# A hybrid streaming encoder step on one core: the gate's projection is transposed into another PSUM bank

## The chip, the cores and the metric

The kernel runs on one core of one Trainium2 chip. TensorE (PE in the profile) multiplies and transposes, VectorE (DVE) and ScalarE (ACT) read what it leaves in PSUM, GpSimd (POOL) does small work on SBUF, and SyncE (SP) starts the transfers. They run side by side and wait for each other through semaphores. The metric is the device time of one execution in microseconds (us).

## What is computed

The layer normalizes x, projects it, and runs three mixers side by side. The change lies in the attention part, in its gate `ag`:

```python
h = rmsnorm(x, norm_g)
proj = h @ w_in
aq, ak, av, ag, gq, gk, gv, gg, glr, cv, cgl, cg = jnp.split(proj, offsets, axis=-1)
q = rmsnorm(aq.reshape(B, L, ATTN_HEADS, HEAD_DIM), q_g)
k = rmsnorm(ak.reshape(B, L, ATTN_KV_HEADS, HEAD_DIM), k_g)
y_attn = band_attention(q, k_all, v_all, sinks, q_pos0) * jax.nn.silu(ag)
y_gla, y_conv = ...
y = jnp.concatenate([y_attn, y_gla, y_conv], axis=-1) @ w_out
return x + y
```

There are 2048 prompt frames and 64 sample frames of width 1024. Matmuls are made in pieces of a high and a low part (`hi`, `lo`) of each operand: hi·hi + hi·lo + lo·hi.

## The kernel before

The work has two passes. The first makes the attention (projections q, k and v, gate, softmax, its half of the output projection) for 17 tiles of 128 frames, `t.n` from 0 to 16 (`LAST`). The second, from about 500 us on, makes the other two mixers for blocks of 256 frames. Nothing of the second pass is touched.

In the first pass each engine has its own `body_a(t)`, called for t = -2 to 17; its code order is its order of work, and only semaphores tie the engines together. PSUM has eight banks: `J` 0 to 2 for projections and outputs, `S` 0 and 1 for scores and the attention's result, `T` 0 to 2 for transposes. TensorE's order in a tile t is:

1. transposes of q (`qkn`) into `T[2]` (L1808) and of k into `T[0]` (L1810);
2. the first half of the q projection of tile t+1, 12 matmuls 512 wide (L654);
3. four transposes of the gate's projection `agraw` (L1821), which this text calls the gate transposes;
4. the other 12 matmuls of that projection;
5. `scores(0)` and `scores(1)` (L1838), the k/v projection of t+1, `scores(2)` and `scores(3)`, the gate projection of t+1 (24 matmuls);
6. `pT(0)`: probabilities into `T[0]` (L1871); `pX()`: the middle probabilities into `T[1]` (L1880);
7. `out(0)` for tile t-1 (12 matmuls, L669), `pv(0)` (L1894 to L1896), `pT(1)` into `T[2]`, `spread_rinv(t + 2)` into `T[1]` (L591), `out(1)`, `pv(1)`.

`spread_rinv` transposes the spread norm factor of a later tile into `T[1]`; ScalarE copies it out in `take_rinv` (L596) and adds 1 to `rb_taken`. After transposes of q, ScalarE copies the high part out of `T[2]` (`qT`, L958), and VectorE subtracts it to make the low part (L1303, adding 1 to `qk_lo` for each of two halves). They do the same for k from `T[0]` (L1062, L1259). Then come v (L968, L1311), the tanh of the gate on ScalarE (L972), and on VectorE the last low part of y of the tile before (L1250) and the gate's product (L1320, `gate_ready`). Only then does VectorE add the bias and take the maxima of the scores (L1270, `nmx` in L1276), on which ScalarE's exponentials (L988) wait. After the softmax's division (L1360) VectorE makes two steps of the next tile's q/k norm (L1368, L1370), and then the low parts of the transposed probabilities (`ptlo`, L1377, and `px`, L1383), on which `pv(0)` waits.

Of the kernel before, what the change touches and what calls it, by code (L numbers as in the profile page):

```python
# [24 lines left out]
ALU = mybir.AluOpType  # L25
ACT = mybir.ActivationFunctionType
# [7 lines left out]
P = 128  # L34
# [5 lines left out]
TILES = SEQ // P + 1  # L40
# [68 lines left out]
def need(eng, sem, count):  # L109

    if isinstance(count, int) and count <= 0:
        return
    eng.wait_ge(sem, count)
# [7 lines left out]
def groups(b):  # L121

    if b < 0 or b >= NB:
        return []
    return [(0, 0, 256, (0, 1)), (1, 256, DEC, (2,))] if b == 0 else [(b + 1, 0, 256, (0, 1))]
# [67 lines left out]
def build(nc, ins, consts, x_T, outs):  # L193
# [7 lines left out]
    def sb(name, shape, dt=F32, ctx=es):  # L201
        return ctx.enter_context(nc.sbuf_tensor(name, shape, dt))

    def sem(name):
        return es.enter_context(nc.semaphore(name))

    with es:
# [33 lines left out]
        agraw = sb("agraw", [P, 512], F32, ea)  # L241
        gth = sb("gth", [P, 512], F32, ea)
# [82 lines left out]
        T = [es.enter_context(nc.psum_tensor(f"T{i}", [P, 512], F32)) for i in range(3)]  # L325
# [36 lines left out]
        rb_psum, rb_taken, x_normed = sem("x_rinv_psum"), sem("x_rinv_taken"), sem("x_normed")  # L362
# [7 lines left out]
        qk_hi, qk_lo = sem("qkT_hi"), sem("qkT_lo")  # L370
        gate_psum, gate_tanh, gate_ready = sem("gate_psum"), sem("gate_tanh"), sem("gate_ready")
# [249 lines left out]
        def key_slots(t):  # L621

            return slice(0, 3, 2) if t.par == 0 else slice(1, 2)
# [10 lines left out]
        def half_rows(i):  # L634

            return slice(i * HD, (i + 1) * HD)
# [286 lines left out]
        def _(act):  # L923
# [9 lines left out]
            def body_a(t):  # L933
# [20 lines left out]
                if t.real():  # L954

                    act.wait_ge(qk_psum, 2 * t.n + 1)
                    for i in range(2):
                        nc.scalar.activation(qT[half_rows(i), :, :, i, :],  # L958
                                             T[2][half_rows(i), :].rearrange("p (h c q) -> p h c q", c=2, q=CHUNK),
                                             ACT.Copy).then_inc(qk_hi, 1)  # L960
                    act.wait_ge(qk_psum, 2 * t.n + 2)
                    if t.n == LAST:
                        act.wait_ge(c_psum, 1)
                    key_hi(slice(0, P), key_slots(t))
                    if t.n == LAST:
                        key_hi(slice(P, 2 * P), slice(1, 2))
                    act.wait_ge(A.taken[1], t.n + 1)
                    nc.scalar.activation(vcat[t.par][:, :, 0:HD], raw[:, 640:768].rearrange("p (h d) -> p h d", d=HD),  # L968
                                         ACT.Copy).then_inc(v_hi, 1)
                    act.wait_ge(gate_psum, t.n + 1)  # L970
                    need(act, y_gated, 2 * t.n)
                    nc.scalar.activation(gth[:, :], T[2][:, :], ACT.Tanh, scale=0.5).then_inc(gate_tanh, 1)  # L972
                    act.wait_ge(v_lo, t.n + 1)
                    for c, src in enumerate((vcat[t.par], vcat[1 - t.par])):
                        nc.scalar.activation(vdup[c][half_rows(1 - c), :, :], src[half_rows(c), :, :],
                                             ACT.Copy).then_inc(v_dup, 1)
# [46 lines left out]
                if t.real():  # L1023
# [6 lines left out]
                    for u in P_ACT:  # L1030
                        nc.scalar.activation(unit(u), unit(u), ACT.Copy,
                                             scale=rden[:, u:u + 1]).then_inc(p_ready[1], 1)
# [24 lines left out]
            def key_hi(cols, slots):  # L1057

                for g in range(KVH):
                    for o in range(2):  # L1060
                        dst = kT[half_rows(o), g, o, slots, :]
                        nc.scalar.activation(dst, T[0][half_rows(g), cols].unsqueeze(1).to_broadcast([HD, dst.shape[1], P]),  # L1062
                                             ACT.Copy).then_inc(qk_hi, 1)

            def cache_v_hi():

                nc.scalar.activation(vcat[1][:, :, 0:HD], ckv[:, 1, :].rearrange("p (h d) -> p h d", d=HD),
                                     ACT.Copy).then_inc(cv_hi, 1)

            over_tiles(act, body_a)  # L1070

            def o_square(g):
# [96 lines left out]
            for b in range(NB + 1):  # L1169
# [47 lines left out]
                if b == NB - 1:  # L1217
                    g = groups(b)[0]
# [10 lines left out]
        def _(dve):  # L1229
# [32 lines left out]
            def body_a(t):  # L1262
                t1, t2 = t + 1, t + 2

                def scores_max(n):

                    for c in range(2):
                        u = 2 * n + c
                        cols = slice((2 - c) * CHUNK if t.n == 0 else 0, BAND)
                        nc.vector.tensor_tensor_reduce(  # L1270
                            out=unit(u)[:, cols], in0=S[n % 2][:, c * BAND:(c + 1) * BAND][:, cols],
                            in1=bias[:, n, cols], scale=1.0, scalar=sinks[:, n:n + 1],
                            op0=ALU.add, op1=ALU.max, accum_out=mx[:, u:u + 1]).then_inc(s_max, 1)

                def scores_neg(n):
                    nc.vector.tensor_scalar(nmx[:, 2 * n:2 * n + 2], mx[:, 2 * n:2 * n + 2], -1.0, None,  # L1276
                                            ALU.mult).then_inc(s_neg, 1)
# [37 lines left out]
                if t.real():  # L1315

                    need(dve, pt_psum, 3 * t.n)
                    dve.wait_ge(s_psum, 4 * t.n + 1)
                    dve.wait_ge(gate_tanh, t.n + 1)
                    nc.vector.scalar_tensor_tensor(gth[:, :], gth[:, :], 1.0, T[2][:, :], ALU.add,  # L1320
                                                   ALU.mult).then_inc(gate_ready, 1)
                    scores_max(0)
                    dve.wait_ge(s_max, 8 * t.n + 2)
                    dve.wait_ge(s_psum, 4 * t.n + 2)
                    scores_neg(0)
                    scores_max(1)
                    dve.wait_ge(s_max, 8 * t.n + 4)
                    scores_neg(1)
# [102 lines left out]
                if t.fixed and t.n == 0:  # L1431
                    split_lo(A, 3 * KT, 3 * KT + STAGES)

            over_tiles(dve, body_a)

            def history(b):
# [202 lines left out]
            for b in range(NB + 1):  # L1639
# [93 lines left out]
                elif b == NB - 1:  # L1733
                    g = groups(b)[0]
# [32 lines left out]
        def _(pe):  # L1767
# [19 lines left out]
            def body_a(t):  # L1787
# [16 lines left out]
                if t.real():  # L1804
                    need(pe, pt_lo, 4 * t.n)
                    pe.wait_ge(n_step, 4 * t.n + 4)
                    for n in range(PAIRS):
                        last = nc.tensor.transpose(T[2][:, n * P:(n + 1) * P], qkn[:, n * P:(n + 1) * P], ident[:, :])  # L1808
# [7 lines left out]
                if t1.real() and t.n > 0:  # L1816
                    project(A, t1, 0, empty_bank("in", t1.n, 0), 0)
                if t.real():
                    pe.wait_ge(qk_lo, 6 * t.n + 2)
                    for j in range(4):  # L1820
                        last = nc.tensor.transpose(T[2][:, j * P:(j + 1) * P], agraw[:, j * P:(j + 1) * P],  # L1821
                                                   ident[:, :])
                    last.then_inc(gate_psum, 1)
                if t.n == LAST:
# [35 lines left out]
                def p_wait(u):  # L1860
                    e = 1 if u in P_ACT else 0
                    mine = (P_DVE, P_ACT)[e]
                    pe.wait_ge(p_ready[e], len(mine) * t.n + mine.index(u) + 1)

                def pT(g):
                    if g == 1:
                        pe.wait_ge(gate_ready, t.n + 1)
                    for n in (2 * g, 2 * g + 1):
                        for c in range(2):
                            p_wait(2 * n + c)  # L1870
                            last = nc.tensor.transpose(T[2 * g][:, c * 256 + n % 2 * P:c * 256 + n % 2 * P + P],  # L1871
                                                       sc[:, n, c * 256:c * 256 + P], ident[:, :])
                    last.then_inc(pt_psum, 1)

                def pX():
                    pe.wait_ge(rb_taken, min(t.n + 2, TILES))
                    for n in range(PAIRS):
                        p_wait(2 * n)
                        p_wait(2 * n + 1)
                        last = nc.tensor.transpose(T[1][:, n * P:(n + 1) * P], sc[:, n, P:2 * P], ident[:, :])  # L1880
                    last.then_inc(pt_psum, 1)
# [22 lines left out]
                if t.real():  # L1904
                    pT(0)
                    pX()
                out(0)
                if t.real():
                    pv(0)
                    pT(1)  # L1910
                when(t + 2, spread_rinv)
                out(1)
                if t.real():
                    pv(1)

            over_tiles(pe, body_a)

            def project_v(b, i):
# [331 lines left out]
```

## Time and profile before

| | |
|---|---|
| median of 3 runs | 1002.54 us (1002.08 to 1003.2) |
| profiled execution, its own time | 1004.64 us |
| its span, first to last instruction | 1002.9 us |
| mean granted TensorE clock | 0.968 of full speed |
| TensorE busy | 929.5 us (93%) |
| VectorE, ScalarE, GpSimd busy | 790.3, 474.3, 201.1 us |
| 16 DMA engines | q1 26.5% of their span |

The profile is one execution. Busy time alone does not tell what sets the end; the timeline (what ran when, with the idle time before an instruction and who ended it in brackets) and the waits do. TensorE's matmuls overlap: a matmul 512 wide is shown as 0.40 us long while the next starts 0.23 us after it. So a true stall is read from start to start.

### The profile page before, as it was taken

The numbers are of one execution on the slowest core, as the hardware profiler recorded it, in microseconds if no ns is written. First come the engines' busy times: TensorE is split into PE (matmuls) and PEld (weight loads), VectorE is DVE, ScalarE is ACT, GpSimd is POOL, SyncE is SP. The second block draws the span as 40 slices with busy tenths as digits, with TensorE's granted clock in tenths as the row PEclk, the third lists the DMA queues.
The fourth block names the chain that finished last, engine by engine and source line by source line (L and its number), as shares of the span: only waits on it lengthen the run. The fifth ranks groups of instructions, "written<-read, shape, count | busy, mean of one in ns | idle before, by whom it ended". The sixth has DMA issues, their size and how long they took to land.

```text
span 1002.9 us, 15973 instructions
## 1 busy us (share of the span) xinstructions
PE 929.5 (93%) x5713; PEld 818.5 (82%) x5713; DVE 790.3 (79%) x1905; ACT 474.3 (47%) x1166; POOL 201.1 (20%) x250
## 2 busy tenths in 40 slices
PE   5759999999999999998997987999999999999987
PEld 4647888888888888886986886998989898998965
DVE  6578878887888787879878668788888887888974
ACT  7366666666666666657634143041422415142311
POOL 0412222222222222220021221020202112120310
PEclk9879999999999999999999788999999999999989
DMA  9323222222223222135332103204021211203021
GB/s 303 123 97 118 106 106 95 106 106 106 106 106 106 105 106 85 65 111 137 104 107 74 44 22 106 84 1 126 1 89 38 75 53 53 75 8 120 1 74 55
DMA packets 57839, 87.79 MB, mean 88 GB/s; under 512 B 10048, under 2 KB 34496, under 8 KB 57760
## 3 DMA queue, kind: packets, MB, share of 16 engines
q1 hardware_dynamic: 57760, 86.77, 26.5%
q8 instruction: 46, 0.75, 0.3%
q14 instruction: 33, 0.27, 0.1%
HBM read 60.21 MB, written 26.60 MB: 87 GB/s over the span
## 4 chain that ended last, share of the span: by engine, by line
PE 65%; DVE 22%; ACT 5%; issue 3%; DMA 2%; POOL 1%; SPq 1%; POOLq 0%; DVEq 0%; ACTq 0%
PE J L1783 17%; PE J L654 16%; PE J L1942 9%; DVE acc L1460 6%; PE J L669 4%; PE J L1927 4%; DVE osum L1395 3%; PE S L1838 3%; DVE osum L1391 2%; DVE qT L1303 2%; ACT olo L1004 2%; DVE wlo L470 1%; PE S L2096 1%; DVE ptlo L1377 1%; PE T L1821 1%
## 5 line engine op out<-in xcount | busy, mean ns | idle before, releaser
L1460 DVE SCALAR_TENSOR_TENSOR acc<-ub,cwh,acc 128x256 f32<-128x256 f32 (+1 forms) x480 | 224.1, 531 | 0.2
L654 PE MATMUL J<-whi,xhi 128*128 128x512 f32 (+1 forms) x408 | 151.1, 370 | 10.5 <-DVE wlo L470 10.5
L1783 PE MATMUL J<-xbh,whi 128*128 128x256 f32 (+1 forms) x512 | 151.8, 296 | 4.5 <-issue 4.5
L1783 PE MATMUL J<-xbl,whi 128*128 128x256 f32 (+1 forms) x512 | 148.0, 289 | 0.0
L1783 PE MATMUL J<-xbh,wlo 128*128 128x256 f32 (+1 forms) x512 | 147.7, 289 | 0.0
L654 PE MATMUL J<-wlo,xhi 128*128 128x512 f32 (+1 forms) x408 | 147.0, 360 | 0.0
L654 PE MATMUL J<-whi,xlo 128*128 128x512 f32 (+1 forms) x408 | 146.9, 360 | 0.0
L1783 PEld LDWEIGHTS J<-xbh,whi 128*128 128x128 f32 x512 | 98.8, 193 | 7.6 <-issue 7.1
L1783 PEld LDWEIGHTS J<-xbl,whi 128*128 128x128 f32 x512 | 98.8, 193 | 0.2
L1783 PEld LDWEIGHTS J<-xbh,wlo 128*128 128x128 f32 x512 | 98.7, 193 | 0.0
L654 PEld LDWEIGHTS J<-whi,xhi 128*128 128x128 f32 x408 | 78.0, 191 | 22.3 <-DVE xlo L612 9.9
L654 PEld LDWEIGHTS J<-whi,xlo 128*128 128x128 f32 x408 | 77.5, 190 | 12.6
L654 PEld LDWEIGHTS J<-wlo,xhi 128*128 128x128 f32 x408 | 78.0, 191 | 10.3
L988 ACT ACTIVATE sc<-sc,nmx 128x192 f32<-128x192 f32 x136 | 60.2, 445 | 19.5 <-DVE nmx L1276 19.5
L1270 DVE CUSTOM_DVE_ANT_0 sc<-S,bias,sinks 128x192 f32<-128x192 f32 (+2 forms) x136 | 50.2, 406 | 19.3 <-PE S L1838 19.3
L669 PE MATMUL J<-whi,yhi 128*128 128x512 f32 x136 | 56.5, 415 | 0.0
L669 PE MATMUL J<-wlo,yhi 128*128 128x512 f32 x136 | 53.7, 395 | 0.0
L669 PE MATMUL J<-whi,ylo 128*128 128x512 f32 x136 | 53.6, 394 | 0.0
L602 POOL TENSOR_TENSOR xraw<-xraw,rb 128x1024 f32<-128x1024 f32 x17 | 40.8, 2400 | 46.3 <-ACT rb L596 46.3
L885 POOL TENSOR_TENSOR oms<-oss,eps_h 128x8 f32<-128x8 f32 (+1 forms) x9 | 4.9, 549 | 179.9 <-DVE oss L1473 179.0
L1927 PE MATMUL J<-whi,xbh 128*128 128x272 f32 x136 | 40.9, 301 | 0.0
L1927 PE MATMUL J<-whi,xbl 128*128 128x272 f32 x136 | 40.2, 296 | 0.0
(270 smaller groups left out, 2270.3 us busy)
## 6 DMA issues: line engine op xcount, KB each, us to landing
out<-res SPq DMA_DIRECT2D x60, 256.0 KB, 2.0
x_normed_scratch<-xraw SPq DMA_DIRECT2D x17, 512.0 KB, 2.9
xraw<-xT SPq DMA_DIRECT2D x16, 512.0 KB, 3.5
xtok<-in_x_prompt SPq DMA_DIRECT2D x16, 512.0 KB, 3.6
res<-in_x_prompt SPq DMA_DIRECT2D x16, 512.0 KB, 4.5
xbraw<-x_normed_scratch SPq DMA_DIRECT2D x16, 512.0 KB, 5.1
res<-out SPq DMA_DIRECT2D x14, 512.0 KB, 4.2
wraw<-in_w_in SPq DMA_DIRECT2D x52, 128.0 KB, 2.5
```

The costliest lines, as they stand in the source:

```text
L602: nc.gpsimd.tensor_tensor(xraw[t.par][:, :, :], xraw[t.par][:, :, :], rb[:, :].unsqueeze(1).to_broadcast([P, KT, P]), ALU.mult).then_inc(x ...
L654: last = nc.tensor.matmul(bank[:, 0:width], x[x_slot(ps, t)][:, k, :], w, start=(k == 0 and n == 0), stop=(k == KT - 1 and n == 2))
L669: last = nc.tensor.matmul(bank[:, :], y[:, k, :], w, start=(k == 0 and n == 0), stop=(k == 3 and n == 2))
L988: last = nc.scalar.activation(unit(u), unit(u), ACT.Exp, bias=nmx[:, u:u + 1], accum_out=esum[:, u:u + 1])
L1004: nc.scalar.activation(olo[:, :], S[g][HD:P, :], ACT.Copy).then_inc(o_low, 1)
L1270: nc.vector.tensor_tensor_reduce(out=unit(u)[:, cols], in0=S[n % 2][:, c * BAND:(c + 1) * BAND][:, cols], in1=bias[:, n, cols], scale=1.0, ...
L1395: nc.vector.scalar_tensor_tensor(osum[:, 2 * g:2 * g + 2, :], osum[:, 2 * g:2 * g + 2, :], 0.5, gth[:, 256 * g:256 * g + 256].rearrange("p ...
L1460: nc.vector.scalar_tensor_tensor(acc[:, j, 0:frames], src, w, acc[:, j, 0:frames], ALU.mult, ALU.add).then_inc(conv_step, 1)
L1783: last = nc.tensor.matmul(bank[:, 0:w], wt, x[:, k, 0:w], start=(k == 0 and m == 0), stop=(k == KT - 1 and m == 2))
L1838: last = nc.tensor.matmul(S[n % 2][:, c * BAND:(c + 1) * BAND], qT[:, n, c, :, :].rearrange("p e q -> p (e q)"), band(t, n // 2, o, c), st ...
L1927: last = nc.tensor.matmul(bank[:, 0:B.widths[1]], x[:, k, at:at + P], wt, start=(k == 0 and m == 0), stop=(k == KT - 1 and m == 2))
L1942: last = nc.tensor.matmul(bank[:, :], y[:, k % 2, at:at + P], wt, start=(k == 0 and m == 0), stop=(k == 3 and m == 2))
```

## The change

Every tile's gate transposes go to `T[1]` in place of `T[2]`, and the two readers follow. Three waits of TensorE move with them.

```diff
@@ scalar engine
                     act.wait_ge(gate_psum, t.n + 1)
                     need(act, y_gated, 2 * t.n)
-                    nc.scalar.activation(gth[:, :], T[2][:, :], ACT.Tanh, scale=0.5).then_inc(gate_tanh, 1)
+                    nc.scalar.activation(gth[:, :], T[1][:, :], ACT.Tanh, scale=0.5).then_inc(gate_tanh, 1)
@@ vector engine
-                    nc.vector.scalar_tensor_tensor(gth[:, :], gth[:, :], 1.0, T[2][:, :], ALU.add,
+                    nc.vector.scalar_tensor_tensor(gth[:, :], gth[:, :], 1.0, T[1][:, :], ALU.add,
                                                    ALU.mult).then_inc(gate_ready, 1)
@@ tensor engine
                 if t.real():
-                    pe.wait_ge(qk_lo, 6 * t.n + 2)
+                    pe.wait_ge(rb_taken, min(t.n + 2, TILES))
                     for j in range(4):
-                        last = nc.tensor.transpose(T[2][:, j * P:(j + 1) * P], agraw[:, j * P:(j + 1) * P],
+                        last = nc.tensor.transpose(T[1][:, j * P:(j + 1) * P], agraw[:, j * P:(j + 1) * P],
                                                    ident[:, :])
                     last.then_inc(gate_psum, 1)
...
                 def pT(g):
-                    if g == 1:
-                        pe.wait_ge(gate_ready, t.n + 1)
                     for n in (2 * g, 2 * g + 1):
...
                 def pX():
-                    pe.wait_ge(rb_taken, min(t.n + 2, TILES))
+                    pe.wait_ge(gate_ready, t.n + 1)
                     for n in range(PAIRS):
```

No instruction is added, removed or put in another order on any engine; only waits and the bank differ.

## Rows read from the trace of the kernel before

**Rows 1.** The page's busy time of each engine in us.

```profile
PE 929.5 (93%) x5713; PEld 818.5 (82%) x5713; DVE 790.3 (79%) x1905; ACT 474.3 (47%) x1166; POOL 201.1 (20%) x250
```

**Rows 2.** Waits: whole span, then 113 to 440 us; total us, times, longest us.

```profile
PE T L1821 <- DVE qT L1303: 14.4, 16, 2.3
...
PE T L1821 <- DVE qT L1303: 8.5, 12, 0.7
```

**Rows 3.** Timeline of TensorE around the gate transposes of tile 9.

```profile
285.25 0.40 PE L654 MATMUL J<-wlo,xhi 128*128 128x512 f32 x1
285.48 0.40 PE L654 MATMUL J<-whi,xlo 128*128 128x512 f32 x1
286.58 0.66 PE L1821 MATMUL T<-ident,agraw 128*128 128x128 f32 x4 [0.71 <-DVE qT L1303]
287.00 0.48 PE L654 MATMUL J<-whi,xhi 128*128 128x512 f32 x1
```

**Rows 4.** Timeline of tile 9: VectorE, TensorE's first scores, ScalarE's copy of the factor.

```profile
285.12 1.41 DVE L1303 TENSOR_TENSOR qT<-T,qT 64x512 fp32r<-64x512 f32 x2
286.56 1.25 DVE L1259 TENSOR_TENSOR kT<-T,kT 64x128 fp32r<-64x128 f32 x4
...
289.50 0.42 DVE L1250 TENSOR_TENSOR ylo<-osum,yhi 128x256 fp32r<-128x256 f32 x1 [1.37 <-ACT yhi L1054]
290.56 0.69 DVE L1320 SCALAR_TENSOR_TENSOR gth<-gth,T 128x512 f32<-128x512 f32 x1 [0.64 <-PE S L1838]
...
289.88 1.03 PE L1838 MATMUL S<-kT,qT 128*128 128x192 f32 x8
...
279.62 0.27 ACT L596 ACTIVATE rb<-T 128x128 f32<-128x128 f32 x1
```

**Rows 5.** Timeline of tile 10 on VectorE, ScalarE and TensorE.

```profile
312.73 1.78 DVE L1259 TENSOR_TENSOR kT<-T,kT 64x256 fp32r<-64x256 f32 x4
...
316.69 0.69 DVE L1320 SCALAR_TENSOR_TENSOR gth<-gth,T 128x512 f32<-128x512 f32 x1
...
325.89 0.82 DVE L1370 TENSOR_REDUCE qss<-qkn 128x10 f32<-128x640 f32 x1
327.46 0.69 DVE L1377 TENSOR_TENSOR ptlo<-T,pthi 128x512 fp32r<-128x512 f32 x1 [0.76 <-ACT pthi L994]
328.18 1.41 DVE L1383 TENSOR_TENSOR px<-T,px 64x512 fp32r<-64x512 f32 x2
...
318.29 0.46 ACT L988 ACTIVATE sc<-sc,nmx 128x192 f32<-128x192 f32 x1 [0.50 <-DVE nmx L1276]
...
316.01 1.03 PE L1838 MATMUL S<-kT,qT 128*128 128x192 f32 x8
...
326.63 0.60 PE L1880 MATMUL T<-ident,sc 128*128 128x128 f32 x4
329.86 0.28 PE L1894 MATMUL S<-pthi,vcat 128*128 128x256 f32 x1
```

**Rows 6.** Timeline of tiles 0 to 2 on TensorE, and VectorE's gate product of tile 1.

```profile
42.76 1.11 PE L1821 MATMUL T<-ident,agraw 128*128 128x128 f32 x4 [2.01 <-DVE qT L1303]
...
75.89 0.66 PE L1821 MATMUL T<-ident,agraw 128*128 128x128 f32 x4 [2.29 <-DVE qT L1303]
...
89.81 0.90 PE L1871 MATMUL T<-ident,sc 128*128 128x128 f32 x4 [0.29 <-DVE sc L1360]
...
103.64 0.66 PE L1821 MATMUL T<-ident,agraw 128*128 128x128 f32 x4 [0.91 <-DVE qT L1303]
...
79.86 0.69 DVE L1320 SCALAR_TENSOR_TENSOR gth<-gth,T 128x512 f32<-128x512 f32 x1 [0.63 <-PE S L1838]
```

**Rows 7.** Busy time by stretch: us, PE, PEld, DVE, ACT, POOL, granted clock, DMA, GB/s.

```profile
40.70:47.60 6.90, 4.89 (x15) 3.96 (x15) 3.36 (x7) 5.46 (x12) 0.00 (x0) 0.51 0.71 232
...
71.50:470.80 399.30, 381.69 (x2187) 325.30 (x2186) 323.24 (x845) 265.58 (x689) 93.85 (x116) 1.00 0.31 105
```

**Rows 8.** Timeline of TensorE: `pv(0)` of tile 15.

```profile
460.95 0.38 PE L1894 MATMUL S<-pthi,vcat 128*128 128x256 f32 x1 [0.26 <-DVE px L1383]
```

## The prediction

> **What bounds the kernel now.** I read the page's busy times first: TensorE is busy in 93% of the span, VectorE in 79% [rows 1]. That alone only says that TensorE is the one to watch. The waits say more. In the regular part of the first pass, 113 to 440 us, TensorE has one wait in the whole list: the gate transposes wait for VectorE's low part of q, 12 times for 12 tiles, 8.5 us in all [rows 2]. So TensorE sets the pace there, and each stall of it lengthens the span unless another wait takes it over. Over the whole span this wait comes 16 times for the 17 tiles, 14.4 us [rows 2]; tile 16 has none, since a whole projection of the second pass stands before its gate transposes.
>
> The reason lies in the bank. `T[2]` still holds q when the gate transposes come, and VectorE reads it until 286.53 in tile 9 (285.12 + 1.41) [rows 3, 4]. The transposes start at 286.58. How much is lost? The view shows 0.71 us idle, but a matmul's end is drawn later than the moment at which the next can start: two matmuls here start 0.23 us apart and are drawn 0.39 to 0.40 long [rows 3]. The last matmul before the gap starts at 285.48, so the transposes could have started at 285.71. The loss is 286.58 - 285.71 = 0.87 us per tile, not 0.71.
>
> **The removed wait.** The reader is to follow TensorE 0.87 us ahead of itself in tile 9 and ask at each later step whether its input is there.
>
> The new wait of the gate transposes is for ScalarE's copy of the spread factor. It ends at 279.89 [rows 4], 5.82 us before 285.71. It costs nothing, and would do so until the copy came 5.82 us later.
>
> `scores(0)`, at 289.88 now, would start at 289.01. It needs the low part of k, done at 287.81 in tile 9 [rows 4]. Tile 10 has two slots of k to fill and is the tighter one: k is done at 314.51, the scores start at 316.01 and would start at 315.14 [rows 5]. 0.63 us are left. The wait does not move here.
>
> VectorE's product of the gate then waits 0.64 us for the scores in tile 9 and not at all in tile 10 [rows 4, 5]. So VectorE gives 0.64 us of the 0.87 in odd tiles and nothing in even ones: in these, the softmax comes 0.87 us later with respect to TensorE. I therefore keep tile 10's VectorE and ScalarE where they are in time, and move TensorE alone. Behind the gate product stand the maxima, the first exponential at 318.29, and the rest of ScalarE's chain; VectorE ends this stretch with the q/k norm's reduction at 326.71 (325.89 + 0.82) [rows 5]. It starts that after it has made the last probabilities, so these are ready some 1.6 us earlier (two steps of 0.82), at about 325.1. `pX` moves from 326.63 to 325.76: 0.6 us to spare.
>
> Next are the transposed probabilities. `ptlo` waits 0.76 us for ScalarE now [rows 5]. It starts at 327.46, would be due at 326.59, and VectorE is free at 326.71: about 0.13 us late. `ptlo` and `px` take from 327.46 to 329.59 now, 2.13 us, so from 326.73 they end at 328.86. `pv(0)` would be due at 329.86 - 0.87 = 328.99 [rows 5]. It fits, with 0.1 us or less after the 0.05 us that a semaphore takes (286.53 to 286.58 in tile 9 [rows 3, 4]). From here on VectorE is again timed by TensorE and the next tile starts as before.
>
> So a middle tile gains the whole 0.87 us, but an even tile has nearly nothing left over. Tiles 3 to 14: 12 x 0.87 = 10.4 us.
>
> **The other two waits that move.** `pX` now waits for `gate_ready`. The gate product is done at 291.25 in tile 9 and 317.38 in tile 10, over 8 us before `pX` [rows 4, 5]; it would have to be 8 us late to cost anything. `pT(1)` no longer waits for it, which gives nothing for the same reason. Behind `pX` are queued `out(0)`, `pv(0)` and all else of TensorE, so a late gate would be dear, but it is not late. ScalarE's tanh comes right behind the gate transposes and waits for them now; the copies after it wait for VectorE's v, so its earlier start is worth nothing. POOL's and SP's queues are not touched.
>
> **The edge tiles.** Here the price is less plain. Tile 2 stalls 0.91 us in the view; with the same 0.16 us that the view hides (0.87 - 0.71) it is 1.07 [rows 3, 6]. I count 1.07.
>
> Tile 1 stalls 2.29 us in the view [rows 6]. Its gate product waits 0.63 us for the scores [rows 6], so the softmax can come 0.63 us earlier at once, and `pT(0)` at 89.81 already waits for it. The whole 2.3 cannot pass. The lower bound is 0.63, the upper 2.3; part of the softmax in this tile hangs on the later scores, which do come earlier, and I take 0.9.
>
> Tile 0 stalls 2.01 us [rows 6], and all behind it waits for the scores. The lower bound is about 1.1: from 40.7 to 47.6 us the granted clock is 0.51, which is the 1.2 GHz level [rows 7], so work brought forward into this stretch runs at half speed. The stall's end at 42.76 lies inside. If the 2.0 us are filled with work at half speed, only half of it is gained. If the clock rises sooner because TensorE did more, the gain could be 2.8. I take 2.0.
>
> On this the Trainium skill's page "TensorE: Matmul & The Clock Gate", section "What's actually happening", says that the gated state is the default and that activity releases it. The trace agrees in kind: with TensorE busy in 381.69 of 399.30 us the clock stays at 1.00, 2.4 GHz, from 71.5 to 470.8 us [rows 7]. By that rule tile 0 would give the 2.8 and the sum below would be 0.8 us larger.
>
> Tile 15 ends differently: VectorE and ScalarE also split the second pass's first weights there, and `pv(0)` already waits 0.26 us for `px` [rows 8]. So only what the gate product gives, 0.64 us as in the other odd tiles [rows 4], gets through. Tile 16 gives 0.
>
> **The sum.** 10.4 + 1.07 + 0.9 + 2.0 + 0.64 = 15.0 us. The second pass and its transfers start from work that moves as a whole, so the gain is kept to the end. The profiled execution took 1004.64 us, its sum is 989.6. The median of the runs is 2.1 us lower, 1002.54, so I predict 987.5 us.
>
> **Rivals.**
>
> *VectorE closes in even tiles.* The margin before `pv(0)` in tile 10 is 0.1 us or less, worked out from rounded rows. If something I have not seen is 0.3 us longer, six even tiles give 0.6 in place of 0.87: 1.6 us less. In the extreme they give nothing, 6 x 0.87 = 5.2 less: 992.7 us. For it speaks that VectorE runs without a pause from the gate product to the second set of maxima; against it, that it then waits for TensorE's `scores(2)` in every tile, which absorbs small delays. Chance 0.13 for between 989.5 and 993.
>
> *The wait moves to the low part of k.* Then TensorE stands before `scores(0)`. With 0.63 us of margin this needs k 0.63 us later than now; 1.5 us later, all is given back and the time is 1002.5. Nothing in the change makes k later. Chance 0.04.
>
> *The change gives more.* If the clock rises sooner in tiles 0 and 1, both gain in full: 0.8 and 1.4 us more, 985.3. If stretches at half clock in the second pass fall more favourably, another 1 us. Chance 0.13 for below 986.
>
> *Slower: the new wait bites.* The gate transposes now wait for ScalarE's copy of the spread factor, the last but few of its steps in a tile. If that copy came later than the low part of q does today, TensorE would stand longer than before. It decides at 286.53 - 279.89 = 6.64 us of delay; each us beyond costs 1 us in 12 or more tiles, so 1 us beyond gives about 1015. Against it: the copy hangs only on TensorE's own transpose, issued a whole `out(1)` and `pv(1)` earlier. Chance 0.02.
>
> *No effect* because TensorE's clock is granted less when it has no pauses: filling the gaps raises the busy share, and if each tile had one stretch of 1.7 us at half clock the 0.87 would be used up. The row from 71.5 to 470.8 shows no such fall at a busy share of 96% [rows 7], so 0.02 is what I leave it.
>
> **How the numbers follow.** Forecast (986 to 989.5) 0.66, more gain 0.13, less gain by VectorE 0.13, wait moved to k 0.04, clock 0.02, slower 0.02. A measurement of this kernel can tell about 0.2%, 2 us, from no change. The first three cases are all faster by over 1%; k gives half faster, half the same. So faster 0.94, same 0.04, slower 0.02. The range of 8 in 10 cuts the tails of the second and third: 984.8 to 991.5 us.
>
> **What would show it right or wrong.** In the profile after: no wait before the gate transposes in tiles 1 to 15, and these 0.23 us after the matmul before; tiles 25.26 us apart in the middle, where they are 26.13 now (316.01 - 289.88 [rows 4, 5]); the gate product no longer waiting for the scores in odd tiles (0.64 to 0); `ptlo`'s wait falling from 0.76 towards 0 in even tiles; no new wait at `scores(0)` or `pv(0)`. A wait of `pv(0)` on `px` in even tiles would show the first rival, one of `scores(0)` on `kT` the second. In tile 1 I expect a larger wait at `pT(0)`, 0.29 + 1.5 or so. The prediction is wrong if any of these new waits adds up to more than 3 us over the pass.

## The result

| | before | after |
|---|---|---|
| median | 1002.74 us (1002.08 to 1003.2, 4 runs) | 986.45 us (983.97 to 987.71, 4 runs) |
| profiled execution: own time, span | 1004.64, 1002.9 us | 983.97, 982.2 us |
| ratio | | 0.9841, 95% interval 0.9828 to 0.9854 |

The forecast was 987.5 us, in a range from 984.8 to 991.5. By the ratio the change saves 15.9 us (14.6 to 17.2); the two medians lie 16.3 us apart. Gains below go by the ratios, unless medians are named. No ratio counts one execution of the kernel before that took 1822.77 us, the only one of all that fell out of line.

First the page of the kernel after, to set beside [rows 1]: busy time of each engine.

```profile
PE 921.1 (94%) x5713; PEld 814.9 (83%) x5713; DVE 792.3 (81%) x1905; ACT 475.2 (48%) x1166; POOL 201.7 (21%) x250
```

Not one instruction is fewer. The list of waits that answers to [rows 2], restricted to TensorE and to 105 to 420 us, is empty after the change: no wait large enough for the view is left in tiles 3 to 14. (A smaller one is, in tile 8, as shown below.) Over the whole span no wait at the gate transposes (L1821) is left. From 30 to 480 us the largest and the third largest waits of TensorE are these (total us, times, longest us).

```profile
PE T L1869 <- DVE sc L1360: 6.3, 3, 4.8
...
PE S L1892 <- DVE px L1383: 3.4, 3, 2.5
```

L1869 and L1892 are `pT` and `pv` (L1871 and L1894 before).

The gate transposes of tile 9 in TensorE's timeline, to set beside [rows 3]:

```profile
273.27 0.40 PE L654 MATMUL J<-wlo,xhi 128*128 128x512 f32 x1
273.50 0.39 PE L654 MATMUL J<-whi,xlo 128*128 128x512 f32 x1
273.74 0.60 PE L1821 MATMUL T<-ident,agraw 128*128 128x128 f32 x4
274.09 0.48 PE L654 MATMUL J<-whi,xhi 128*128 128x512 f32 x1
```

They start 0.24 us after the matmul before, in place of 1.10 us. There is a second, smaller gain. The four transposes keep TensorE for 0.35 us (273.74 to 274.09), where it was 0.42 behind the stall (286.58 to 287.00 in [rows 3]). So the stall cost 0.87 + 0.06 = 0.93 us.

VectorE is now where the time is short. Its timeline in tile 10, to set beside [rows 5], with TensorE's transposes and scores of that tile:

```profile
303.75 0.69 DVE L1320 SCALAR_TENSOR_TENSOR gth<-gth,T 128x512 f32<-128x512 f32 x1
...
306.49 0.42 DVE L1270 CUSTOM_DVE_ANT_0 sc<-S,bias,sinks 128x192 f32<-128x192 f32 x1 [0.23 <-PE S L1838]
...
312.99 0.82 DVE L1370 TENSOR_REDUCE qss<-qkn 128x10 f32<-128x640 f32 x1
313.72 0.68 DVE L1377 TENSOR_TENSOR ptlo<-T,pthi 128x512 fp32r<-128x512 f32 x1
314.43 1.41 DVE L1383 TENSOR_TENSOR px<-T,px 64x512 fp32r<-64x512 f32 x2
...
298.93 0.60 PE L1821 MATMUL T<-ident,agraw 128*128 128x128 f32 x4
302.17 1.03 PE L1838 MATMUL S<-kT,qT 128*128 128x192 f32 x8
```

Where `ptlo` waited 0.76 us, it now follows the reduction without a pause. `px` ends at 315.84, and `pv(0)` starts at 316.02. The wait before the third pair of maxima (L1270, for `scores(2)`) shrank from 1.17 us in the timeline of before to 0.23.

In one middle tile TensorE does stand at `pv(0)` (L1892). This is tile 8:

```profile
264.05 1.41 DVE L1383 TENSOR_TENSOR px<-T,px 64x512 fp32r<-64x512 f32 x2
...
264.82 0.40 PE L669 MATMUL J<-wlo,yhi 128*128 128x512 f32 x1
265.05 0.39 PE L669 MATMUL J<-whi,ylo 128*128 128x512 f32 x1
265.51 0.38 PE L1892 MATMUL S<-pthi,vcat 128*128 128x256 f32 x1
```

`pv(0)` starts 0.46 us after the matmul before it, where 0.23 is the pitch, and `px` ended 0.05 us before it, at 265.46 (264.05 + 1.41). So 0.23 us are lost, of which the drawn ends hide all but 0.07. The repeated kernel below has the same 0.23 in tile 8.

To see where the 20.7 us between the two spans come from, I take the start of `pv(0)` in each tile (L1894 before, L1892 after) from the timelines, and the difference of its distances:

| stretch | before | after | gained |
|---|---|---|---|
| tile 0, q transposes to `pv(0)` | 23.53 | 19.11 | 4.42 |
| `pv(0)` of tile 0 to tile 1 | 30.81 | 29.95 | 0.86 |
| tile 1 to 2 | 26.44 | 25.33 | 1.11 |
| tile 2 to 14 | 313.61 | 302.85 | 10.76 |
| tile 14 to 15 | 26.54 | 25.96 | 0.58 |
| tile 15 to 16 | 32.53 | 33.28 | -0.75 |
| tile 16 to the end | 509.38 | 506.12 | 3.26 |

The last two rows lie where nothing was changed, and tile 0 gave twice what I counted. The experiments had to say which of this is the change.

### The profile page after: what moved, and what is told of

Its sections match the earlier page's. It is cut to its first block, busy times and chain, and to the rows that moved or that the text cites. A ratio compares the mean times of both kernels' runs of the same rounds, so it can differ in the third digit from the quotient of the medians.

```text
span 982.2 us, 15956 instructions
## 1 busy us (share of the span) xinstructions
PE 921.1 (94%) x5713; PEld 814.9 (83%) x5713; DVE 792.3 (81%) x1905; ACT 475.2 (48%) x1166; POOL 201.7 (21%) x250
## 4 chain that ended last, share of the span: by engine, by line
PE 74%; DVE 15%; ACT 5%; issue 3%; DMA 2%; POOL 1%; SPq 1%; POOLq 0%; DVEq 0%; ACTq 0%
PE J L654 19%; PE J L1783 17%; PE J L1940 9%; PE J L669 8%; DVE acc L1460 6%; PE J L1925 4%; PE S L1838 2%; PE T L1869 1%; ACT sc L988 1%; PE S L2094 1%; PE T L2022 1%; DMA wraw<-in_w_in 1%; PE S L1892 1%; DVE wlo L470 1%; PE J L1962 1%
## 5 line engine op out<-in xcount | busy, mean ns | idle before, releaser
L654 PEld LDWEIGHTS J<-whi,xhi 128*128 128x128 f32 x408 | 77.8, 191 | 20.7 <-DVE xlo L612 9.7
L654 PEld LDWEIGHTS J<-wlo,xhi 128*128 128x128 f32 x408 | 77.8, 191 | 10.4
L988 ACT ACTIVATE sc<-sc,nmx 128x192 f32<-128x192 f32 x136 | 60.3, 445 | 11.5 <-DVE nmx L1276 11.5
L1270 DVE CUSTOM_DVE_ANT_0 sc<-S,bias,sinks 128x192 f32<-128x192 f32 (+2 forms) x136 | 50.2, 406 | 8.8 <-PE S L1838 8.6
L1925 PE MATMUL J<-whi,xbh 128*128 128x272 f32 x136 | 40.7, 299 | 0.0
L1783 PE MATMUL J<-xbh,w2hi 128*128 128x256 f32 (+1 forms) x128 | 37.6, 294 | 3.1 <-ACT cgate L1103 3.1
```

Source lines behind the costliest of these rows:

```text
L654: last = nc.tensor.matmul(bank[:, 0:width], x[x_slot(ps, t)][:, k, :], w, start=(k == 0 and n == 0), stop=(k == KT - 1 and n == 2))
L988: last = nc.scalar.activation(unit(u), unit(u), ACT.Exp, bias=nmx[:, u:u + 1], accum_out=esum[:, u:u + 1])
L1270: nc.vector.tensor_tensor_reduce(out=unit(u)[:, cols], in0=S[n % 2][:, c * BAND:(c + 1) * BAND][:, cols], in1=bias[:, n, cols], scale=1.0, ...
L1783: last = nc.tensor.matmul(bank[:, 0:w], wt, x[:, k, 0:w], start=(k == 0 and m == 0), stop=(k == KT - 1 and m == 2))
L1925: last = nc.tensor.matmul(bank[:, 0:B.widths[1]], x[:, k, at:at + P], wt, start=(k == 0 and m == 0), stop=(k == KT - 1 and m == 2))
```

## The experiments

Eleven more runs were made, two of them of the changed kernel itself. Ratios are against the kernel before on the same chip.

**The change again.** No edit.

> The changed kernel once more, to see how its starts and its second pass differ from one execution to the next. My theory: the gate wait is the whole cause, worth 0.93 us in each middle tile whatever the execution; so tiles 3 to 14 take 10.8 us less than before again, and pv(0) of tile 14 stands about 17 us earlier than in the trace of before. What lies behind tile 15 (2.5 us of the first trace's 20.7) may come out otherwise, since only the granted clock differs there. Median 985 to 988 us, ratio 0.982 to 0.985. Rival: the second pass really got faster by the change; then its 2.5 us are there again.

Measured: 986.65 us (985.4 to 987.14), ratio 0.9843 (0.9825 to 0.9862). Its own trace repeats the stretches that the change touches: 19.12, 29.99, 25.35, 302.94 and 25.96 us. From tile 15 to 16 it has 32.50 us, and from there to the end 509.26, as before the change. So the 3.26 us of the first trace's second pass are not the change's. Over all thirteen traces that stretch takes 505.9 to 509.4 us, and kernels without the change lie near both ends of this too (509.38 before, 506.42 before with more VectorE work, below). What differs with it is the granted clock. This is the stretch behind `pv(0)` of tile 16 in the busy times (us, then PE, PEld, DVE, ACT, POOL, clock, DMA share, GB/s), first in the trace after the change:

```profile
476.10:982.20 506.10, 475.62 (x3187) 430.76 (x3185) 405.85 (x919) 152.57 (x348) 90.31 (x105) 0.97 0.20 62
```

and in that of the repeated kernel:

```profile
476.10:985.30 509.20, 480.47 (x3187) 435.33 (x3185) 405.07 (x919) 152.40 (x349) 89.53 (x105) 0.96 0.20 62
```

TensorE is busy 4.85 us longer with the same 3187 matmuls. The tie is loose: with 0.42 us more of VectorE work (below) the stretch is the shortest of all, 505.92 us, with TensorE busy for 477.7.

**The bank without the freedom.** Gate transposes in `T[1]`, but the old wait kept in front of the new one:

```diff
+                    pe.wait_ge(qk_lo, 6 * t.n + 2)
                     pe.wait_ge(rb_taken, min(t.n + 2, TILES))
```

> The gate transposes still go to the other bank, but TensorE waits for VectorE's low part of q as before, on top of the new wait. My theory (only that wait counts, the bank itself and the two other moved waits are worth nothing): all is given back, 1001 to 1004 us, ratio 0.998 to 1.002, and the wait of 0.71 us is back in every middle tile. Rival (another bank is worth something of its own, since the readers of the two banks no longer meet, or the two waits moved at pX and pT(1) give something): 2 us or more stay gained, below 1000.5 us.

Measured: 1002.1 us (1000.32 to 1003.94, 10 runs), ratio 0.9998 (0.9985 to 1.0011). The rival needed 2 us of gain to be left, and the interval allows 1.5 at most. The timeline of TensorE in tile 9 has the stall back:

```profile
284.70 0.39 PE L654 MATMUL J<-whi,xlo 128*128 128x512 f32 x1
285.81 0.66 PE L1822 MATMUL T<-ident,agraw 128*128 128x128 f32 x4 [0.72 <-DVE qT L1303]
286.23 0.47 PE L654 MATMUL J<-whi,xhi 128*128 128x512 f32 x1
```

Tile 2 to 14 takes 313.60 us, as before the change. The other bank, the waits moved to `pX` and away from `pT(1)`: together worth nothing, within 1.5 us by the runs and within 0.1 us in the middle tiles. The one wait is the gain.

**Tiles 0 and 1 alone, and tiles 2 to 16 alone.** A function `moved(t)` chooses bank and waits per tile, in both kernels:

```diff
+        moved = lambda t: t.n < 2          # the other kernel: t.n >= 2
+        gate_bank = lambda t: T[1] if moved(t) else T[2]
...
-                    pe.wait_ge(rb_taken, min(t.n + 2, TILES))
+                    if moved(t):
+                        pe.wait_ge(rb_taken, min(t.n + 2, TILES))
+                    else:
+                        pe.wait_ge(qk_lo, 6 * t.n + 2)
...
                 def pT(g):
+                    if g == 1 and not moved(t):
+                        pe.wait_ge(gate_ready, t.n + 1)
...
                 def pX():
-                    pe.wait_ge(gate_ready, t.n + 1)
+                    if moved(t):
+                        pe.wait_ge(gate_ready, t.n + 1)
+                    else:
+                        pe.wait_ge(rb_taken, min(t.n + 2, TILES))
```

> The bank is changed for tiles 0 and 1 alone; the others are as before. By the trace of the changed kernel tile 0 gives 4.4 us (2.2 of the wait and 2.2 since the projection behind it no longer runs at the lower clock) and tile 1 0.9: 5.3 us, 997.3 us, ratio 0.9947. As I predicted tile 0 (2.0 us, no change of clock) it would be 2.9 us, 999.7. If the granted clock at 40 us varies from one execution to the next on its own, the kernel before has the fast start at times too, and the gain lies between.

> The bank is changed for tiles 2 to 16; tiles 0 and 1 are as before. Tile 2 gives 1.1 us, tiles 3 to 14 10.8, tile 15 0.6, tile 16 nothing: 12.5 us, 990.2 us, ratio 0.9875, and together with the kernel that changes tiles 0 and 1 alone the two gains make up that of the whole change within 1.5 us. Rival (tiles interact: VectorE's lateness is carried on): the two gains differ from the whole by more than 3 us.

Measured: tiles 0 and 1 alone 998.09 us (995.83 to 999.13), ratio 0.9953 (0.9936 to 0.9969), a gain of 4.7 us. From tile 2 on 990.46 us (989.64 to 991.89), ratio 0.9885 (0.9865 to 0.9904), 11.5 us. I had expected 5.3 (or 2.9 without a change of clock) and 12.5. Together they make 16.2 us, the whole is 15.7 to 15.9. Each of the two intervals reaches 1.6 to 2.0 us to either side, so the times alone would not rule out the rival's 3 us. The traces do. With tiles 0 and 1 as before, tile 2 to 14 takes 302.91 us, and 302.85 and 302.94 with the whole change; with only tiles 0 and 1 changed, tile 0 to 1 takes 29.99 us, as in the whole change. The parts add up, and VectorE's lateness is not carried from tile to tile.

With tiles 0 and 1 alone changed, tile 0 took 20.78 us, not 19.11. The busy times from 40.5 to 47.5 us tell why. Kernel before, kernel after, tiles 0 and 1 alone, and the kernel with the wait kept:

```profile
40.50:47.50 7.00, 4.99 (x16) 3.88 (x15) 3.36 (x7) 5.47 (x12) 0.00 (x0) 0.52 0.70 228
```

```profile
40.50:47.50 7.00, 6.72 (x35) 5.45 (x33) 4.05 (x9) 5.34 (x12) 0.16 (x1) 1.00 0.69 226
```

```profile
40.50:47.50 7.00, 7.00 (x28) 5.77 (x28) 3.36 (x7) 5.55 (x12) 0.00 (x0) 0.79 0.72 226
```

```profile
40.50:47.50 7.00, 4.98 (x18) 4.07 (x18) 3.36 (x7) 5.56 (x12) 0.00 (x0) 0.76 0.70 226
```

In the same 7 us TensorE makes 16, 35 and 28 matmuls in the first three, at a granted clock of 0.52, 1.00 and 0.79; before, it also stood still for 2 us of them. Three traces without the change in tile 0 (before, wait kept, tiles 2 to 16) have 22.92 to 23.53 us for this stretch. Four with it (the kernel after three times, tiles 0 and 1 alone) have 19.11, 19.12, 20.66 and 20.78. So tile 0 gives 2.1 to 4.4 us, 3.4 by the means.

The clock here is not a matter of the change alone. The fourth row has the stall and still a clock of 0.76, and the three traces of the kernel after have 1.00, 1.00 and 0.76. Where both sides have about the same clock (22.92 us at 0.76 with the stall, 20.66 at 0.76 and 20.78 at 0.79 without) tile 0 gives 2.1 to 2.3 us, which is the stall itself. What goes beyond that is the clock. Over all thirteen traces it is 0.51 to 0.76 in the five with the stall and 0.76 to 1.00 in the eight without. So it tends to be higher without the stall, but how much of that is owed to the change stays open.

**How much room VectorE has left.** One more VectorE instruction per tile, which adds constants into a spare buffer between the gate product and the first maxima; nothing reads it. In three widths W: 256 columns (0.42 us), 512 (0.69), 768 (0.95).

```diff
                                                    ALU.mult).then_inc(gate_ready, 1)
+                    if t.n == 0:
+                        dve.wait_ge(ident_loaded, 16)
+                    cs = ident[:, :].unsqueeze(1).to_broadcast([P, W // P, P])
+                    nc.vector.tensor_tensor(spare[:, 0:W].rearrange("p (c n) -> p c n", c=W // P), cs, cs, ALU.add)
                     scores_max(0)
```

> The kernel before with one more VectorE instruction per tile (an addition of 128x512 into a buffer that nobody reads, about 0.69 us) between the gate product and the first maxima of the scores. My theory: in the kernel before TensorE stood 0.87 us at the gate transposes, after which VectorE had 1 us of room before pv(0) even in even tiles, so the middle tiles take it for nothing; only tiles 0, 1 and 15 pay 0.69 us each and tile 16 some 0.4: 2.5 us, 1004.7 us, ratio 1.0025. Rival (VectorE was at its limit in every tile before the change too): 17 x 0.69 = 11.7 us, ratio 1.0117.

> The changed kernel with 0.42 us more of VectorE at the same place (128x256). By the trace of the changed kernel pv(0) in even tiles has 0.11 us of room, in odd ones 0.6: even tiles 4 to 14 pay 0.3 each (1.8 us), odd ones nothing, and tiles 0, 1, 2 and 15 pay 0.42 (1.7 us): 3.5 us over the changed kernel, 990.0 us, ratio to before 0.988. Rival (TensorE sets the pace with room to spare): 1.3 us, ratio 0.9855.

> The changed kernel with the 0.69 us instruction. My theory: even tiles 4 to 14 pay 0.55 each (3.3 us), odd ones 0 to 0.1, tiles 0, 1, 2, 15 pay 0.69 and tile 16 some 0.4 (3.2 us): 6.5 to 7 us over the changed kernel, 993.3 us, ratio to before 0.991; in its trace pv(0) waits for px in even tiles by some 0.5 us. The same instruction costs more than twice as much as in the kernel before. Rival (margins as before): 2.5 us over the changed kernel, 989, ratio 0.987.

Measured: before with 0.69 us 1003.68 us, ratio 1.0013 (1.0003 to 1.0023), 1.3 us where I expected 2.5; after with 0.42 us 989.29, ratio 0.9872 (0.9857 to 0.9887), near the 990.0 expected; after with 0.69 us 989.16, ratio 0.9870 (0.9857 to 0.9883). The changed kernel did not run on this chip, so the costs below set medians of two chips side by side. By the medians this is a miss for my theory: I expected 6.5 us for 0.69, it cost 2.7, as much as 0.42 did, and that is the rival's number. The traces of the same kernels say otherwise. From tile 2 to 14 the kernel before stays at 313.62 us, while the kernel after goes from 302.85 to 303.99 and 305.61. With 0.69 us an even tile takes 25.64 us for 25.20, and 0.09 more is lost on the way to the next one, so 0.53 per even tile; over the twelve tiles it is 2.76 us. Two readings contradicted each other, so I took a larger dose, with a control on the same chip.

> The changed kernel again, as the control of the two runs beside it on the same chip: 985 to 987.5 us. Its trace: 25.21 us from tile to tile in the middle, no wait of TensorE there; the part from pv(0) of tile 16 to the end between 505.9 and 509.4 us, as in the eight traces so far.

> The changed kernel with one VectorE instruction of 0.95 us (128x768) per tile between the gate product and the first maxima. With 0.69 us the traces showed 0.52 us lost in each even tile and nothing in odd ones, but the medians only 2.7 us over the changed kernel, where I had expected 6.5. My theory (VectorE is at its limit in even tiles): even tiles 4 to 14 lose 0.52 + 0.27 = 0.79 each, odd ones up to 0.2, tiles 0, 1, 2, 15 some 0.9: 4.7 + 0.6 + 3.6 = 9 us over the control, by the medians 7 to 10. Rival (the traces overstate it, VectorE has room): 3.5 us or less over the control.

> The kernel before with the same 0.95 us instruction. Its even tiles had 0.87 us of waiting at the gate transposes and 0.1 more before pv(0), so the middle tiles take 0.95 us for nothing or nearly so; tiles 0, 1, 15 and 16 pay as with 0.69 us, somewhat more: 2 to 4 us, ratio to before 1.002 to 1.004. Rival: as much as in the changed kernel.

Measured: control 985.92 us (984.24 to 987.82), ratio 0.9845 (0.9830 to 0.9860). After with 0.95 us 995.81 (995.2 to 996.71), ratio 0.9945 (0.9931 to 0.9959): 9.9 us over the control, expected 9. Before with 0.95 us 1005.52, ratio 1.0042 (1.0029 to 1.0054): 3.9 us, expected 2 to 4. From tile 2 to 14 the kernel before stands at 313.64, still nothing lost; the kernel after at 308.57, 5.7 us more than the control's 302.87. The same instruction costs two and a half times as much after the change.

Where does TensorE stand then? I had said at `pv(0)`, by some 0.5 us in even tiles. That was wrong. This is TensorE in tile 10 of the kernel after with 0.69 us:

```profile
311.08 0.61 PE L1842 MATMUL S<-kT,qT 128*128 128x192 f32 x4
311.86 0.69 PE L1842 MATMUL S<-kT,qT 128*128 128x192 f32 x4 [0.18 <-DVE mx L1270]
...
321.45 0.39 PE L669 MATMUL J<-whi,ylo 128*128 128x512 f32 x1
321.68 0.36 PE L1896 MATMUL S<-pthi,vcat 128*128 128x256 f32 x1
321.88 0.28 PE L1897 MATMUL S<-ptlo,vcat 128*128 128x256 f32 x1
```

L1842 is `scores(2)` and `scores(3)`. Without the extra instruction `scores(3)` starts 0.43 us after `scores(2)`; here it is 0.78, and its second matmul comes late by 0.09 more. Together 0.44 us, all that the even tile loses before its `pv(0)`. The wait is for the maxima of `scores(1)`, which must have left the bank. `pv(0)` (L1896) starts 0.23 us after the matmul before it, so it is not late at all; only its second matmul is, 0.20 us behind the first in place of 0.12. With 0.42 us `scores(3)` starts 0.11 late, so it had about 0.3 us of room.

The waits of the kernel after with 0.95 us, 113 to 430 us, seem to name both places alike. PEld rows are the weight loads, which start early and so wait first:

```profile
PEld S L1842 <- DVE mx L1270: 3.5, 12, 0.3
PEld S L1896 <- DVE px L1387: 3.4, 13, 0.3
PE S L1842 <- DVE mx L1270: 1.1, 6, 0.2
```

From start to start they are not alike: in tile 10, which takes 26.03 us there for 25.20, some 0.73 us are lost at `scores(2)` and `scores(3)` and 0.10 at a `pv(0)`. I had not checked the scores. What the 0.69 us dose really cost over many executions stays open between 2.7 us (medians) and 4.6 us (traces, tile 0's `pv(0)` to tile 15's); a difference of that size is within what the clock of the second pass moves.

**A version that beats both.** Tile 0 is the only one in which TensorE makes the gate projection of the next tile before its scores, and then waits 4.76 us for the softmax. Half of it is moved behind:

```diff
                 if t.n == 0:
-                    project(A, t1, 2, empty_bank("in", t1.n, 2))
+                    project(A, t1, 2, empty_bank("in", t1.n, 2), 0)
...
                     scores(2)
                     scores(3)
+                if t.n == 0:
+                    project(A, t1, 2, bank_of("in", t1.n, 2), 1)
```

> The changed kernel, and in tile 0 the second half of the gate projection of tile 1 (12 matmuls) comes after the scores instead of before them. TensorE waits 4.76 us for the softmax in tile 0 and could make these 12 matmuls (2.8 us) there; the scores start earlier, but no sooner than the low part of k is there, 1.25 us before they start now. My theory: 1.25 us less than the changed kernel, 985.2 us, ratio to before 0.983. Rival (the granted clock in tile 0 falls, since TensorE stands longer before the scores): nothing gained or 1 us lost, 986 to 988.

Measured: 984.49 us (981.81 to 985.04, 5 runs), ratio 0.9812 (0.9798 to 0.9827), against 0.9841 to 0.9845 for the changed kernel in its three comparisons, none of them on this chip. TensorE's timeline in tile 0 of the kernel after:

```profile
54.15 1.15 PE L1869 MATMUL T<-ident,sc 128*128 128x128 f32 x4 [4.76 <-DVE sc L1360]
...
58.69 0.58 PE L1892 MATMUL S<-pthi,vcat 128*128 128x256 f32 x1 [2.54 <-DVE px L1383]
```

and of the split one:

```profile
53.43 0.90 PE L1871 MATMUL T<-ident,sc 128*128 128x128 f32 x4 [1.98 <-DVE sc L1360]
...
57.97 0.58 PE L1894 MATMUL S<-pthi,vcat 128*128 128x256 f32 x1 [3.21 <-DVE px L1383]
```

The wait for the softmax falls by 2.78 us, the time of the 12 matmuls. The end of the stretch, from the q transposes at 39.91, comes after 18.06 us for 19.11: 1.05 us gained, near the 1.25 expected, although the first matmuls ran at half clock here (0.43 us apart at 42 us). The medians show 1.4 to 2.2 us less than the changed kernel's three, the ratios 2.9 to 3.3; the interval overlaps with one of the three and ends 0.0001 and 0.0003 below the other two. The size is not settled; that tile 0 became shorter is what the trace shows.

## Why the prediction was right

**The bound.** TensorE sets the pace in the middle of the first pass: right. Keeping the wait alone brought back 1002.1 us.

**0.87 us per middle tile, 10.4 us.** Measured 10.76 for tiles 3 to 14, by 302.85 for 313.61. Reading the loss from start to start, not from the idle shown, gave 0.87; the real figure is 0.93, since the transposes behind a stall also take 0.06 us longer. Over twelve tiles that would be 11.2. Tile 8 gives back 0.23 at `pv(0)`, since a small step of its softmax on VectorE waited 0.35 us longer for ScalarE than in tile 10; the kernel before has the same lateness in that tile and lost nothing by it. The tiles behind tile 8 and behind tile 2, whose `pv(0)` also stood for `px`, are 0.11 longer each.

**No wait takes its place in even tiles, with 0.1 us to spare at `pv(0)`.** Right in five of the six even tiles: `px` ends 0.18 us before `pv(0)` in tile 10, and a semaphore needs 0.05 to 0.06 of it (265.46 to 265.51 in tile 8). In tile 8 the first rival came true: 0.23 us were lost at `pv(0)`. In odd tiles the gate product no longer waits for the scores (277.98 us in tile 9, right behind the step before). This step left out a limit: `scores(3)`, which needs the maxima of `scores(1)`, had about 0.3 us of room. All three doses of VectorE work stopped TensorE at the scores, so they show that VectorE has little room left, but they do not test the 0.1 us at `pv(0)` by themselves; that stands on the timeline.

**The moved waits at `pX` and `pT(1)` cost and give nothing.** Right: they give nothing by the kernel with the wait kept, and the list of TensorE's waits after the change has none at `pX`.

**Tiles 1, 2 and 15.** Predicted 0.9, 1.07 and 0.64; measured 0.86, 1.11 and 0.58. In tile 1 the wait moved to `pT(0)` as said, 1.03 us rather than about 1.8: the scores came only 1.6 us earlier, not 2.3. The timeline there:

```profile
84.10 0.90 PE L1869 MATMUL T<-ident,sc 128*128 128x128 f32 x4 [1.03 <-DVE sc L1360]
```

**Tile 0: 2.0 us, between 1.1 and 2.8.** This term was mis-sized: 2.1 to 4.4, in the mean 3.4. I took the granted clock of 0.51 from 40.7 us on as given and let the work brought forward run into it. With the stall gone the lower clock was granted for about half of that stretch or not at all. The rival that the clock rises sooner was right, and its price too low: the 2.8 was given without working, and in two of four traces the clock did not fall in this stretch at all. In part this is the luck of the execution, since one kernel with the stall in place had a clock of 0.76 there. The Trainium skill's page "TensorE: Matmul & The Clock Gate", section "What's actually happening", by which activity releases the throttle, pointed the right way. The traces agree in direction, with 0.51 to 0.76 in the five that have the stall and 0.76 to 1.00 in the eight that do not, but 0.76 stands on both sides. The 2.8 us that the prediction tied to this rule lies within the measured 2.1 to 4.4.

**The sum.** With the measured terms it is 10.76 + 1.11 + 0.86 + 3.4 + 0.58 = 16.7 us for 15.0 predicted; the runs say 15.9 (14.6 to 17.2). The profile's own 20.7 us is more than either: it happened to hit a fast tile 0 and a fast second pass. That the forecast of 987.5 us came within 1.1 of the median, 986.45, owes something to luck: the runs say 0.8 us less than the terms, which made up for a part of tile 0.

## What to carry to other kernels

Size a stall from start to start against the pitch of the instructions before it, and then move the freed engine ahead on paper, tile by tile, until it meets each input: the step with the least room tells whether the gain is whole. Do this for every wait on the way, since each one that had been covered by the stall is a candidate, and for even and odd tiles where they differ: here the wait that bit when VectorE got more work was not the one with the least room on paper, but one left out. An empty list of waits does not show that nothing is lost, since the drawn ends hid most of tile 8's 0.23 us; compare the distances from tile to tile. A gain may use up another engine's room: 0.95 us of extra VectorE work cost 3.9 us before and 9.9 us after.

## What the runs showed of the hardware

The granted clock of TensorE differs between executions of one kernel. From 40.5 to 47.5 us the kernel after has 1.00, 1.00 and 0.76 in its three traces. For the stretch after `pv(0)` of tile 16, in which all kernels have the same instructions in the same order, the thirteen traces have 505.9 to 509.4 us, with TensorE busy between 475.6 and 480.5 us in the rows above. That is up to 0.35% of the whole, as much as some of the effects asked for here; distances within the regular tiles repeat to 0.1 us in 313.6.
